# Expert mixer of a two-layer backbone: the two gather passes over a token tile become one pass in groups of four slots

## What is computed

```
q = (h @ wq).reshape(T, P_HEADS, 2, P_DKEY // 2)
s = jnp.einsum("thpd,hpnd->thpn", q, sub_keys)
sv, si = lax.top_k(s, P_TOPK)
cand = sv[:, :, 0, :, None] + sv[:, :, 1, None, :]
...
fv, fi = lax.top_k(cand, P_TOPK)
gate = softmax(fv)                       # 8 heads x 16 = 128 experts per token
a = gelu(einsum("tkd,td->tk", u_tab[ib], hb)) * gb
out = einsum("tk,tkd->td", a, v_tab[ib])
```

## Time and profile before

| | |
|---|---|
| median of 3 executions | 5850.38 us (5845.36 to 5850.7) |
| span of the profiled execution, first to last instruction | 5667.9 us |
| that execution's own time | not recorded; the median is 182.5 us above the span |
| PE, DVE, ACT, POOL busy, share of the span | 60%, 55%, 15%, 50% |
| software DMA queue (the gathers): bytes, share of 16 engines | 1344.49 MB, 62.0% |
| tile loops: first to last gather | 1090.35 to 3298.88 us (layer 0), 4190.28 to 5649.08 us (layer 1) |

### The profile page before, as it was taken

How to read it: one execution, slowest core, us unless ns; L and a number is a source line. 1 busy time by engine, 2 the same in 40 slices (tenths; PEclk the granted TensorE clock), 3 DMA queues, 4 the chain that set the end, 5 groups by cost and what they waited for, 6 DMA issues and landing times. The chain is left out here.

```text
span 5667.9 us, 44412 instructions
## 1 busy us (share of the span) xinstructions
PE 3406.2 (60%) x10078; PEld 1753.1 (31%) x10088; DVE 3122.1 (55%) x6265; ACT 848.7 (15%) x1873; POOL 2834.4 (50%) x2680
## 2 busy tenths in 40 slices
PE   6987897868339066092480877478572924708329
PEld 1534673643113022030130333255341401303113
DVE  1055432586675865856758321433368577586662
ACT  1012331111002011020110210241110201101001
POOL 0010001277777777777777720100037777777776
PEclk8998658989769588596695988795786967859769
DMA  6141002599999999999999940000279999999999
GB/s 244 45 137 45 0 0 93 199 397 364 370 376 371 342 370 355 384 360 359 366 368 390 376 191 27 4 1 1 101 247 391 372 363 376 369 360 375 384 359 362
DMA packets 534664, 1501.28 MB, mean 265 GB/s; under 512 B 97097, under 2 KB 174441, under 8 KB 533017
## 3 DMA queue, kind: packets, MB, share of 16 engines
q0 software_dynamic: 369312, 1344.49, 62.0%
q1 hardware_dynamic: 112272, 122.88, 6.7%
q10 hardware_dynamic: 52976, 32.84, 1.9%
HBM read 1486.02 MB, written 12.68 MB: 264 GB/s over the span
## 5 line engine op out<-in xcount | busy, mean ns | idle before, releaser
L1632 PE MATMUL ps<-ex_ring,ex_diag 128*128 128x512 f32 x3840 | 1718.7, 604 | 1662.7 <-ACT ex_diag L1578 1597.8
L1418 POOL DMA_INDIRECT ex_ring<-in_p_u,ex_idx x1280 | 1381.6, 1079 | 649.4 <-issue 498.2
L1490 DVE SCALAR_TENSOR_TENSOR ex_product<-ex_ring,H 128x1024 f32<-128x1024 f32 x1280 | 1531.7, 1223 | 300.6 <-issue 160.5
L1418 POOL DMA_INDIRECT ex_ring<-in_p_v,ex_idx x1280 | 1354.4, 1058 | 468.8 <-issue 335.9
L1632 PEld LDWEIGHTS ps<-ex_ring,ex_diag 128*128 128x128 f32 x3840 | 718.5, 192 | 2659.5 <-issue 2545.9
L1511 DVE SCALAR_TENSOR_TENSOR ex_mixed<-ex_ring,ex_weight,ex_mixed 128x1024 f32<-128x1024 f32 x320 | 411.4, 1286 | 924.6 <-DMA ex_ring<-in_p_v,ex_idx 922.6
L1578 ACT ACTIVATE ex_diag<-ident_sb,ex_weight 128x128 f32<-128x128 f32 x960 | 379.9, 401 | 1331.8 <-PE ps L1632 1308.6
L394 PE MATMUL ps<-win_w,hT 128*128 128x384 f32 (+1 forms) x960 | 351.7, 528 | 6.8 <-issue 3.4
L437 POOL TENSOR_TENSOR R<-R,pout_tmp 128x512 f32<-128x512 f32 x20 | 25.3, 1263 | 499.5 <-DVEq L428 499.5
L1608 PE MATMUL ps<-hT,ex_wq 128*128 128x320 f32 (+1 forms) x768 | 238.1, 472 | 28.9 <-DMA ex_wq<-in_p_wq 28.9
L1571 ACT ACTIVATE ex_dots<-ex_dots 128x128 f32<-128x128 f32 x10 | 3.1, 309 | 1585.5 <-DVEq L1497 1585.5
(11 more groups left out here) (274 smaller groups left out, 3233.5 us busy)
## 6 DMA issues: line engine op xcount, KB each, us to landing
mod_w<-in_w_mod SPq DMA_DIRECT2D x12, 2048.0 KB
qk_w<-in_w_mod SPq DMA_DIRECT2D x16, 1536.0 KB, 7.4
ex_ring<-in_p_u,ex_idx POOLq DMA_INDIRECT x1280, 6.3
ex_ring<-in_p_v,ex_idx POOLq DMA_INDIRECT x1280, 6.3
pre_w<-in_p_wq SPq DMA_DIRECT2D x8, 2048.0 KB, 11.8
ex_wq<-in_p_wq ACTq DMA_DIRECT2D x32, 512.0 KB, 11.4
win_w<-in_e_w_in SPq DMA_DIRECT2D x6, 1536.0 KB, 7.3
ex_sc<-key_scores SPq DMA_DIRECT2D x8, 1024.0 KB, 8.5
```

The costliest lines, as they stand in the source:

```text
L1418: pool.indirect_dma_start(ring[:, r, :], None, v_rows if phase else u_rows, bass.IndirectOffsetOnAxis(ap=idx[:, n // IDX, n % IDX:n % IDX ...
L1490: dve.scalar_tensor_tensor(out=product[:, n % 2, :], in0=ring[:, r, :], scalar=1.0, in1=m.H[:, t + t0, :], op0=ALU.mult, op1=ALU.mult, acc ...
L1632: mm = pe.matmul(m.ps[:, b, :], diag[:, k % NDIAG, :], ring[:, r, b * BANK:(b + 1) * BANK], start=False, stop=False, skip_group_check=True)
```

## The change

There is now one pass over the slots of a tile. For each slot GpSimd issues two gathers one after the other, u into the left half of the slot's ring place and v into the right half; the ring has 8 places of 8 KB. The left half is free when VectorE has taken the dot product (`u_read`), the right half when TensorE has used it (`spent`). After every 4 dots (`dotted`) ScalarE applies Gelu to them, multiplies each with its gate (four copies of one column), and makes four diagonal matrices; TensorE then does all 128 slots of the tile. VectorE's share of the v rows, the copies of expert numbers into `idx` and the hardware loops are gone: the code of all tiles is written out. TensorE's sums of even and odd tiles go to different PSUM banks, and VectorE takes the sum of a tile after slot 15 of the next (`take`).

The later scores move into the first tile: before the slots 0, 4, 12, 16, 24, ... 96 (`late_turns`) TensorE does a query product and the previous half head's score product; `wq` has 2 places, `late` has 1, and their loads and stores are issued by SyncE. The key scores of the second tile are loaded in quarters as they become complete. `choose` gives one step after each sixth slot from slot 36 in the first tile and two after each slot from 108 on (`ripe`); in later tiles one after each third slot. The modulation `g` is loaded once for each kind of token, after `wq`.

```diff
-    RING, IDX, BODY = 8, 8, 32
-    VDVE = 3
+    RING, GROUP = 8, 4
...
-        ring = s.sb("ring", [P, RING, D])
-        idx = s.sb("idx", [P, NIDX, IDX], U32)
+        ring = s.sb("ring", [P, RING, 2 * D])
...
-        LPER = 4
+        WQ = 2
...
+        LATE_EVERY = 6
+        def late_turns(t, n):
+            return [hh for hh in range(NH + 1) if t == 0 and LATE_EVERY * hh // GROUP * GROUP == n]
...
+                sp.dma_start(iota[:, :], rows(a["iota"])).then_inc(iota_loaded, 16)
+                sp.dma_start(keysT[:, :, :], m.keysT[:, :, :]).then_inc(keysT_loaded, 16)
+                for hh in range(WQ):
+                    load_wq(hh)
+                load_g(1 if t0 < CT else 0)
+                sp.wait_ge(sc_read, 1)
+                for hh in range(NH):
+                    if hh + WQ < NH:
+                        sp.wait_ge(wq_used[hh % WQ], hh // WQ + 1)
+                        load_wq(hh + WQ)
+                    if hh:
+                        store_late(hh - 1)
+                    if hh % 4 == 1 and hh > 4:
+                        sp.wait_ge(late_stored, 16 * (hh - 1))
+                        load_sc(1, hh // 4 - 1)
+                store_late(NH - 1)
+                sp.wait_ge(late_stored, 16 * NH)
+                load_sc(1, NH // 4 - 1)
...
             @block.gpsimd
+                for t in range(T):
+                    pool.wait_ge(chosen, t + 1)
+                    for n in range(SLOTS):
+                        r, use = n % RING, (t * SLOTS + n) // RING
+                        row = bass.IndirectOffsetOnAxis(ap=expert[:, t % 2, n:n + 1], axis=0)
+                        if use:
+                            pool.wait_ge(u_read[r], use)
+                        pool.sem_inc(claimed, 1)
+                        pool.indirect_dma_start(ring[:, r, 0:D], None, u_rows, row).then_inc(u_landed[r], 16)
+                        if use:
+                            pool.wait_ge(spent[r], use)
+                        pool.sem_inc(claimed, 1)
+                        pool.indirect_dma_start(ring[:, r, D:2 * D], None, v_rows, row).then_inc(v_landed[r], 16)
...
             @block.vector
+                def ripe(t, n):
+                    if t:
+                        return 1 if n % 3 == 2 else 0
+                    if n < LATE_EVERY * (NH + 2):
+                        return 1 if n >= LATE_EVERY * 6 and n % LATE_EVERY == 0 else 0
+                    return 2
...
-                dve.wait_ge(g_loaded, 32)
...
             @block.scalar
+                    for b in range(GROUPS):
+                        for hh in late_turns(t, b * GROUP):
+                            if hh < NH:
+                                late_query(hh)
+                            if hh:
+                                late_score(hh - 1)
+                        act.wait_ge(dotted, t * GROUPS + b + 1)
+                        act.activation(act_w[:, b % 2, :], dots[:, t % 2, b * GROUP:(b + 1) * GROUP], ACT.Gelu)
+                        act.drain()
+                        for k in range(GROUP):
+                            act.activation(weight[:, b % 2, k:k + 1], act_w[:, b % 2, k:k + 1], ACT.Copy,
+                                           scale=gates[:, t % 2, n:n + 1])
+                        act.drain()
+                        for k in range(GROUP):
+                            if use:
+                                act.wait_ge(spent[r], use)
+                            act.activation(diag[:, r, :], m.ident[:, :], ACT.Copy, scale=weight[:, b % 2, k:k + 1])\
+                               .then_inc(diag_ready, 1)
...
             @block.tensor
+                    for n in range(SLOTS):
+                        for hh in late_turns(t, n):
+                            if hh < NH:
+                                late_query(hh)
+                            if hh:
+                                late_score(hh - 1)
+                        r, use = n % RING, (t * SLOTS + n) // RING
                        pe.wait_ge(v_landed[r], use * 16 + 16)
+                        pe.wait_ge(diag_ready, t * SLOTS + n + 1)
+                        for b in range(2):
+                            mm = pe.matmul(mix_banks(t)[:, b, :], diag[:, r, :], ring[:, r, D + b * BANK:D + (b + 1) * BANK],
+                                           start=(n == 0), stop=(n == SLOTS - 1))
+                        mm.then_inc(spent[r], 1)
```

More of the change, by code:

```diff
@@ L1405, in _, with load_g, load_wq, store_late @@
-                tiles_loop(sp, tile)
+                def load_g(stream):
+                    sp.dma_start(g[:, :], rows(m.mods[layer, stream:stream + 1, 5 * D:6 * D])).then_inc(g_loaded, 16)
+                def load_wq(hh):
+                    sp.dma_start(wq[:, hh % WQ], a["p_wq"][layer][:, hh * P:(hh + 1) * P]
+                                 .rearrange("(k p) n -> p k n", p=P)).then_inc(wq_loaded[hh % WQ], 16)
+                def store_late(hh):
+                    sp.wait_ge(late_ready, hh + 1)
+                    sp.dma_start(m.scores[t0 + 1:NT, :, hh * P:(hh + 1) * P].rearrange("t p n -> p t n"),
+                                 late[:, :, :]).then_inc(late_stored, 16)
@@ new lines, in _ @@
+                load_sc(1, NH // 4 - 1)
+                for t in range(1, T):
+                    if t + 1 < T:
+                        sp.wait_ge(sc_read, t + 1)
+                        for q in range(NH // 4):
+                            load_sc(t + 1, q)
+                    if last:
+                        sp.wait_ge(added, t)
+                        sp.dma_start(m.out[0, (t - 1 + t0 - CT) * P:(t + t0 - CT) * P, :],
+                                     m.R[:, t - 1 + t0, :]).then_inc(stored, 16)
+                    if t0 < CT and t == CT - t0:
+                        sp.wait_ge(added, t)
+                        load_g(0)
@@ L1407, in _ @@
+                if last:
+                    sp.wait_ge(added, T)
+                    sp.dma_start(m.out[0, (T - 1 + t0 - CT) * P:(T + t0 - CT) * P, :],
+                                 m.R[:, T - 1 + t0, :]).then_inc(stored, 16)
+                    sp.wait_ge(stored, 16 * T)
             @block.gpsimd
             def _(pool):
[L1409 to L1420 removed]
@@ new lines, in choose, with take @@
+                    dve.sem_inc(weighed, 1)
+                    yield
+                def take(t):
+                    dve.wait_ge(summed, t + 1)
+                    dve.wait_ge(g_loaded, 32 if t0 < CT and t + t0 >= CT else 16)
+                    dve.tensor_tensor(product[:, 0, :], mix_banks(t).rearrange("p b c -> p (b c)"), g[:, :], ALU.mult)\
+                        .then_inc(mix_taken, 1)
+                    dve.drain()
+                    dve.tensor_tensor(m.R[:, t + t0, :], m.R[:, t + t0, :], product[:, 0, :], ALU.add).then_inc(added, 1)
+                    dve.drain()
@@ new lines, in ripe @@
+                def ripe(t, n):
[4 more added lines that the diff above has]
+                    return 2
+                dve.wait_ge(iota_loaded, 16)
+                for _ in choose(0, True):
+                    pass
+                for t in range(T):
+                    steps = choose(t + 1) if t + 1 < T else iter(())
+                    for n in range(SLOTS):
+                        r, use = n % RING, (t * SLOTS + n) // RING
+                        dve.wait_ge(u_landed[r], use * 16 + 16)
+                        dve.scalar_tensor_tensor(out=product[:, n % 2, :], in0=ring[:, r, 0:D], scalar=1.0,
+                                                 in1=m.H[:, t + t0, :], op0=ALU.mult, op1=ALU.mult,
+                                                 accum_out=dots[:, t % 2, n:n + 1]).then_inc(u_read[r], 1)
+                        if n % 2:
+                            dve.drain()
+                        if n % GROUP == GROUP - 1:
+                            dve.sem_inc(dotted, 1)
+                        if t and n == 2 * RING - 1:
+                            take(t - 1)
+                        for _ in range(ripe(t, n)):
+                            next(steps, None)
@@ L1526, in tile @@
-                    dve.drain()
-                    dve.tensor_tensor(m.R[:, t + t0, :], m.R[:, t + t0, :], mixed[:, :], ALU.add).then_inc(added, 1)
-                    dve.drain()
-                dve.memset(zeros[:, :], 0.0).then_inc(zeroed, 1)
-                dve.wait_ge(iota_loaded, 16)
-                dve.wait_ge(g_loaded, 32)
-                for _ in choose(0, True):
-                    pass
-                tiles_loop(dve, tile)
+                take(T - 1)
             @block.scalar
```

279 lines of the change are left out of this document (73 added, 206 removed).

## The result

The changed kernel takes 5956.14 us (median of 4 runs), the kernel before 5848.49 us on the same chip: ratio 1.0181, 95% interval 1.0163 to 1.02. It is 108 us slower; I had forecast 135 us.

A forecast was written before the change was run, and what follows sets the result against it. Gathers were taken to bound the tile loops. The terms -64 + 98 + 43 + 42 + 20 - 20 + 18 = +137 us on 5850 gave 5987, stated as 5985 us; range 5840 to 6160 us for 8 in 10.

The forecast's parts named there:

- Terms 2 and 3: First tiles of layers 0 and 1: late scores between slots lengthen PE's list; +98 and +43 us.
- Term 4: Loads and stores of the late-score turns, first tiles: waits for landings cost +42 us in layer 0, +20 in layer 1.
- the turn: Late query and score between slot groups, first tile: costs PE 12.8 us in layer 0, 8.7 in layer 1.
- The burst: First tile from slot 108: two choose steps per slot hold up VectorE's dots, 55 us for ten slots.
- Term 1: Later tiles: pauses at borders and between passes and the small copies go, 8 us a tile, -64 us.
- best stretch: Fastest gathers in the earlier profile, 1.360 us each at share 1.00, taken as the best pace: 348.3 us a tile.
- Term 5: Round trip of a right half, 12.0 or 13.7 us, fits in 11 gathers' 15.0 us; costs only some later-tile gain.
- Term 6: Ends: earlier starts, with 7 us from not waiting for g, give -20 us; the longer final tail costs +18.
- (b): Rival: first-tile turns hide under the gathers, so the kernel is faster, 5815 us; chance 0.13.
- (c): Rival: PE's lower clock bounds later tiles, 13.6 us a group, about 6270 us; chance 0.12.
- (d): Rival: gains and costs cancel within 12 us, 5850 us; chance 0.07.
- The two tables: Rival tested afterwards: reading u and v tables alternately slows later tiles' gathers; removing it saves 70 us or more.

The follow-up runs named there:

- experiment 6: Changed kernel with ScalarE making a group's weights and diagonals ahead of the late query and score copies; ratio 1.0081 to the kernel before.
- experiment 11: experiment 10 with choose's last 23 steps in two of three slots from slot 85 on; ratio 1.0001 to the kernel before.
- experiment 8: Changed kernel without choose's top-16 searches for the third and later tiles, Exp moved to group 3; ratio 1.0081 to the kernel before.
- experiment 9: Kernel before with only VectorE's wait for g moved behind the first choose; ratio 0.9998 to the kernel before.
- experiment 4: Changed kernel with the second gather of each slot reading u rows instead of v rows; ratio 1.0242 to the kernel before.
- experiment 12: experiment 11 with a fourth late-score turn ahead of slot 0 and the Exp at group 28; ratio 0.9929 to the kernel before.
- experiment 10: experiment 6 with three of 16 late-score turns ahead of slot 0, the others three turns earlier; ratio 1.0054 to the kernel before.
- experiment 5: Changed kernel once more, unchanged, profiled on a fast chip; ratio 1.0207 to the kernel before.

## Why the prediction was right, and where not

Slower, and by about as much as said: +108 us where the result was taken, +116 on the fast chips, against my +137. The mechanism is right in its main part, the first tiles pay more than the later ones gain; that the total came so close is in part luck, since the errors of the terms partly cancel: +11 in the later tiles, -18 in the first ones, -14 at the ends. Term by term, against the +116:

- **Terms 2 and 3, first tiles.** Forecast +98 and +43, with term 4 +140 and +63; measured +113 and +72. The working of the turn held to the row (12.78 us). ScalarE's order within a turn was a dear part: experiment 6 takes 47 and 33 us away by it alone. The burst held in its shape, with waits of PE of 9 to 14 us; from the last score to the tile's end 99 us pass on the fast chip and 101 on the slow one, against my 98 from 376 to 474. In layer 1 it is 99 us too, where I had 90 (320 to 410); that is most of what layer 1 lies above the forecast. Spreading the steps gives back only 9 and 12 of them (experiment 11).
- **Term 4, loads and stores: the step that failed.** The landings of 24 to 30 us were those of queues full of gathers. With gathers held up by PE a load lands in 4.3 us in layer 0 and 9.9 in layer 1, and in both layers ScalarE's copy waits for the score and not for a store. In the place of the 42 us stands 14 us on the fast chip (the last score 390 us behind the first gather, not 376) and 45 us on the slow one (421): PE's lower clock behind pauses (12 us on the fast chip by experiment 6) and, on the slow chip, about 14 us of late score products. In the place of layer 1's 20 us stand 17 (337, not 320) and 29 (349). I had put the lower clock only at the tile's end. On the slow chip layer 0's term came out right for the wrong reason, by luck. What makes those score products late is not settled.
- **Term 1, later tiles.** -64 forecast, -53 measured. The mechanism was half of it: the pauses at the borders are gone, but the best pace is kept away by VectorE's searches, some 15 us a tile (experiment 8), which I hadn't seen. The "best stretch" of the earlier trace rows was the last tile of layer 0, the one that chooses for no next tile.
- **Term 5** held for the round trip: GpSimd waits for PE 30 us in 1200. Steps of choose between dots hold up no engine that a wait shows, but those with searches cost the tiles pace all the same (experiment 8).
- **Term 6, ends.** -2 forecast, -16 measured. The head's 10 us are right, but 3 of them come from g and not 7 (experiment 9). The tails are shorter than I priced: +5 and not +9 at the end, and none is visible between the layers, as far as a stretch tells that differs by 7 us between two profiles of the kernel before.
- **Rivals.** (b) fell: the turns don't hide, their list is longer than the tile. (c) fell: later tiles have a mean clock of 0.86 to 0.89, most groups behind a wait do start at the lower level (8.6 to 10 us), but a group has 11 us. (d) fell by the interval. The two tables (experiment 4) have no part in it.

The version of experiment 12, faster than the kernel before on a slow chip, shows what the change was short of: not the single pass, but ScalarE's order within a turn, idle PE ahead of the first slot, and steps of choose held back for the end. Each was undone by itself or beside the others (6, 10, 11), with 67, 25 and 25 us between medians. The 25 of experiment 10 goes across two chips and is 15 by the ratios, not clear of noise; the other two are.

## What to carry to other kernels

When work moves in between a pipeline's slots, add up the whole list of the in-order engine first, and then look at the helper that serves both: what it makes for the next slots must not stand behind its copies for the moved piece. A short pause can be paid twice on TensorE, as a wait and as slower matmuls behind it. Take landing times from a stretch in which the queues are as full as they will be.

## What the runs showed of the hardware

- The kernel before takes 5661.5, 5665.4 and 5662.4 us in three groups on two chips, and 5848.5 and 5844.3 in two others: 3.2% apart. Later tiles of layer 0 of the changed kernel move 375 GB/s at share 0.99 on a fast chip and 360 at 0.97 on a slow one. Ratios differ less: 1.0207 (1.0181 to 1.0233) and 1.0181 (1.0163 to 1.02).
- VectorE's searches (max, find index, match replace) beside gathers take 4% of their pace: 366.2 us a tile with them, 350.9 without (experiment 8).
- Over two short pauses around a score product, 2.91 and 2.37 us at 1245 to 1252 us, PE fell to the lower of its two levels, 1.2 GHz: the granted clock is 1.00 from 1240 to 1245 us and 0.50 from 1250 to 1256, and the group takes 10.13 us. In experiment 5 a single pause of 2.37 us has four slots of 8.60 us behind it in one turn and eight at full clock (13.97) in the other. In experiment 6, without pauses, four slots take 7.03.
- Landings follow how full the queues are. In the kernel before, the same 512 KB load from the same queue lands in 4.0 us just ahead of layer 1's first gather (4150 to 4189 us) and in 29.1 beside the gathers. In the changed kernel, whose gathers wait for PE, it is 4.3 in layer 0 and 9.9 in layer 1.

```profile
ex_wq<-in_p_wq ACTq DMA_DIRECT2D x7, 512.0 KB, 4.0
```
